# A block of attention, experts and two hybrid layers: 512-column products with an identity, at the edges of stages

## The reference

```python
def first_block(x, ...):
    z = rms_norm(x, norm1_g) @ w_in
    y_nsa = nsa_attention(...)        # compressed, selected and windowed keys
    y_dil = dilated_attention(...)
    x = x + (gate0 * (y_nsa @ w_up_nsa) + gate1 * (y_dil @ w_up_dil)) @ w_o
    return x + peer(rms_norm(x, norm2_g), ...)      # experts

def hybrid_layer(x, ...):             # twice
    proj = rms_norm_2(x, n_pre_mix) @ w_in
    y_a, y_b, y_c = pool_mixer(...) @ w_a, gla_mixer(...) @ w_b, mla_mixer(...) @ w_c
    merged = gates[0] * y_a + gates[1] * y_b + gates[2] * y_c
    x = x + rms_norm_2(merged @ w_o, n_post_mix)
    gu = rms_norm_2(x, n_pre_ffn) @ w_ffn_gu
    ffn = (silu(gu[..., :D_FF]) * gu[..., D_FF:]) @ w_ffn_down
    return x + rms_norm_2(ffn, n_post_ffn)
```

## Time and profile before

| | |
|---|---|
| median of 3 runs | 3793.26 us (3791.05 to 3793.95) |
| profiled execution | 3793.5 us |
| its span, first to last instruction | 3791.7 us |
| mean granted TensorE clock | 0.969 |
| TensorE busy | 3584.7 us (95%) |
| VectorE busy | 2367.3 us (62%) |
| ScalarE busy | 1422.4 us (38%) |
| GpSimd busy | 391.9 us (10%) |

### The profile page before, as it was taken

One profiled execution on the slowest core, in us unless ns is written; L12 is line 12 of the kernel. 1 busy time (PEld: TensorE's weight loads), 2 busy tenths in 40 slices (PEclk: granted clock), 3 DMA queues, 4 the chain that ended last, 5 costly groups with the idle time before them and its releaser, 6 DMA issues. The chain is left out here.

```text
span 3791.7 us, 47619 instructions
## 1 busy us (share of the span) xinstructions
PE 3584.7 (95%) x18126; PEld 3069.5 (81%) x18133; DVE 2367.3 (62%) x4248; ACT 1422.4 (38%) x2386; POOL 391.9 (10%) x309
## 2 busy tenths in 40 slices
PE   8988999999999899999998989999999898999998
PEld 6666777999999899999886767788878676778886
DVE  3376664889999888888635556554343545564433
ACT  3234343434799543333323324332222322443221
POOL 0020000000244433333000100000000010000000
PEclk9999999999999999999998999999999998999999
DMA  3220232555799999999432224233323222333332
GB/s 129 81 78 23 73 123 84 177 170 174 262 380 379 392 347 381 373 365 368 159 101 69 80 62 136 84 100 100 94 74 100 73 78 59 123 103 92 98 94 70
DMA packets 212358, 597.86 MB, mean 158 GB/s; under 512 B 21730, under 2 KB 79748, under 8 KB 210596
## 3 DMA queue, kind: packets, MB, share of 16 engines
q1 hardware_dynamic: 175268, 460.58, 36.8%
q0 software_dynamic: 36864, 134.23, 9.2%
HBM read 525.00 MB, written 69.21 MB: 157 GB/s over the span
## 5 line engine op out<-in xcount | busy, mean ns | idle before, releaser
L653 ACT ACTIVATE stream_hi<-stream_raw 128x1024 fp32r<-128x1024 f32 (+1 forms) x615 | 642.7, 1045 | 1204.3 <-PE ffn_ps L2773 416.8
L661 DVE TENSOR_TENSOR stream_lo<-stream_raw,stream_hi 128x1024 fp32r<-128x1024 f32 (+1 forms) x615 | 745.1, 1212 | 401.9 <-ACT stream_hi L653 393.2
L1231 PE MATMUL experts_ps<-mix_a_hi,stream_hi 128*128 128x384 f32 x1024 | 342.8, 335 | 18.2 <-issue 16.8
L689 PE MATMUL experts_ps<-h_hi,stream_hi 128*128 128x384 f32 x1024 | 347.9, 340 | 1.5 <-PEq L101 1.5
L689 PE MATMUL experts_ps<-h_hi,stream_lo 128*128 128x384 f32 x1024 | 343.1, 335 | 0.0
L689 PE MATMUL experts_ps<-h_lo,stream_hi 128*128 128x384 f32 x1024 | 343.1, 335 | 0.0
L1231 PE MATMUL experts_ps<-mix_a_lo,stream_hi 128*128 128x384 f32 x1024 | 342.6, 335 | 0.0
L1231 PE MATMUL experts_ps<-mix_a_hi,stream_lo 128*128 128x384 f32 x1024 | 342.5, 334 | 0.0
L2771 PE MATMUL mid_ps<-h_hi,stream_hi 128*128 128x512 f32 x672 | 286.2, 426 | 20.2 <-DVE h_lo L2800 17.1
L2771 PE MATMUL ffn_ps<-h_hi,stream_hi 128*128 128x512 f32 x704 | 283.4, 402 | 17.7 <-DVE h_lo L2800 17.7
L2773 PE MATMUL ffn_ps<-h_hi,stream_lo 128*128 128x512 f32 x704 | 275.4, 391 | 0.0
(11 more groups left out here) (465 smaller groups left out, 7115.5 us busy)
## 6 DMA issues: line engine op xcount, KB each, us to landing
stream_raw<-u SPq DMA_DIRECT2D x128, 512.0 KB
stream_raw<-v SPq DMA_DIRECT2D x128, 512.0 KB
stream_raw<-l_gu SPq DMA_DIRECT2D x88, 512.0 KB
expert_hidden<-experts_gelu SPq DMA_DIRECT2D x128, 192.0 KB
expert_weights<-built SPq DMA_DIRECT2D x12, 2048.0 KB
built<-expert_weights SPq DMA_DIRECT2D x16, 1536.0 KB
built<-expert_hidden SPq DMA_DIRECT2D x128, 192.0 KB
stream_raw<-l_gate SPq DMA_DIRECT2D x48, 512.0 KB
```

The lines of the kernel that those rows point to most:

```text
L653: self.nc.scalar.activation(self.hi[n % self.RING][:, 0:w], self.raw[n % self.RAW][:, 0:w], ACT.Copy).then_inc(self.hi_done, 1)
L661: self.nc.vector.tensor_tensor(self.lo[n % self.RING][:, 0:w], self.raw[n % self.RAW][:, 0:w], self.hi[n % self.RING][:, 0:w].bitcast(F32) ...
L689: mm = self.nc.tensor.matmul(self.ps[n % 2], a, b[:, k, :], start=(k == 0 and m == 0), stop=(k == DC - 1 and m == 2))
L1231: mm = nc.tensor.matmul(out[d][:, DIRECT:SEQ], v, a[b % RING][:, :], start=(b == 0 and m == 0), stop=(b == KEYS - 1 and m == 2))
```

## The change

A new function multiplies the bf16 identity, repeated four times along the free dimension, by the bf16 identity into one bank of PSUM, n times: each product is 128x128 by 128x512. It waits for nothing and raises no semaphore. It is called on TensorE at seven places of the code. `paired_attention` is used twice, and the others once for each of two layers, so the calls run at 14 places, with 183 products in all. The banks are `turned[0]` of the attentions, and banks 3, 6, 2, 5 and 2 of the other stages; what is written there is not read: the next product into them starts anew.

```diff
@@ paired_attention, tensor
                 score(0)
+                idle_products(nc, C, turned[0], 10)
                 for n in range(N):
...
                     mix(n, chunks[n] - 1)
+                idle_products(nc, C, turned[0], 8)
@@ after three
+def idle_products(nc, C, out, n):
+
+    of = C.mask_ident.unsqueeze(1).to_broadcast([P, 4, P])
+    for _ in range(n):
+        nc.tensor.matmul(out.rearrange("p (a c) -> p a c", a=4), C.mask_ident, of, start=True, stop=True)
@@ project, tensor
+                idle_products(nc, C, bank[3], 14 if res.adds else 9)
                 res.first_two(pe, stream, first, bank, total)
@@ merge_and_out, tensor
             def _(pe):
+                idle_products(nc, C, bank[6], 12)
                 for n in range(N_UP):
...
                 leave.total(pe, total)
+                idle_products(nc, C, bank[2], 18)
@@ ffn, tensor
             def _(pe):
+                idle_products(nc, C, bank[5], 14)
                 res.first_two(pe, stream, first, bank, x_total)
...
                 leave.total(pe, m_total)
+                idle_products(nc, C, bank[2], 18)
```

## The result

| | before | after |
|---|---|---|
| median (range, executions) | 3793.61 us (3791.05 to 3798.87, 4) | 3773.79 us (3769.47 to 3775.02, 4) |
| profiled execution | 3793.5 us | 3774.04 us |
| its span | 3791.7 us | 3772.2 us |
| mean granted TensorE clock | 0.969 | 0.979 |

The ratio (changed kernel over kernel before) is 0.9944, 95% interval 0.9931 to 0.9956: faster by 0.56%, 19.8 us on the medians. The prediction said 3781.5 (3775 to 3791).

What follows compares the result with a forecast made beforehand. TensorE, busy 95%, was taken to bound the kernel, losing time to waits and the lower clock. Terms -12.9 + 0.4 + 3.0 - 1.9 - 0.7 + 0.4 = -11.7 from 3793.5 gave 3781.8, stated as 3781.5 us, range 3775 to 3791.

Steps and rivals of the forecast that it cites:

- Starts of merge, feed-forward and second projection: Five stage openings: products hidden in the waits win back the lost clock, 5 x 2.57 = 12.9 us gained, bounds 8.4 and 15.2.
- hidden ends: Four ends of merge and feed-forward: 18 products hidden behind VectorE's reciprocal with no margin, 0.1 us each, +0.4 in all.
- mean of all nine edges: Clock loss in the 8 us after work resumes, averaged: 23.12 / 9 = 2.57 us, used for each of five entries.
- Ends of the attentions: Ends of dil and nsa: nothing covers the 8 products, the next stage starts later, +1.5 us each, +3.0.
- First scores: Waits inside the paired attentions' first scores, ten products each: nsa gains 1.9 us, dil 0.7 (bounds +1.0 and -2.3).
- +1.0 of delay: dil's first scores: ten products at 0.43 us take 4.3 against a wait of 3.31, delaying the next scores by 1.0.
- Start of the first projection: First layer's projection: nine products at the lower clock delay by 2.2 us against at most 2.24 won back; +0.4.
- identity products don't hold the clock: Rival for all edges: clock falls as before and products run at the lower level, +20.5 us, 3814 us; chance 0.10.
- partial: Rival: end products delay each barrier about 1 us, merges' entry sometimes still cold; -2.5, 3791 us; chance 0.15.
- moderate case: Rival: edges at the low bound, 8.4, or first projection and dil at their upper bound; -7.2, 3786 us; chance 0.17.

Runs made afterwards that it cites:

- mixers_later: Kernel before plus 16 identity products at the end of both layers' projections, to start the mixers 2.8 us later; 3799.05 us.
- five_entries: Changed kernel with only the calls at starts and ends of merge and feed-forward and the second projection's start; 3776.91 us, ratio 0.9951.
- mixers_shifted: Changed kernel plus 7 identity products at the end of both projections, to put off the mixers' stages by some 0.8 us; 3781.27 us.
- gla_later: Kernel before plus five unneeded VectorE operations at the end of the first layer's projection, no identity products; 3795.80 us.
- ends_only: Changed kernel with only the 18 products at the ends of merge and feed-forward; 3787.34 us.
- starts_only: Changed kernel without the products at the ends of the attentions, merges and feed-forwards; 3775.79 us.
- no_attention_ends: Changed kernel without the 8 products at the ends of dil and nsa; 3772.52 us, ratio 0.9942.
- before_again: Kernel before, unchanged, run for a second profile; 3795.89 us.
- attentions_only: Changed kernel with only the calls in the two paired attentions, 36 products; 3795.53 us.
- more_edges_2: Changed kernel without products at the attentions' ends, with products at many further edges, up's end and latent's last rotation included; 3753.10 us, ratio 0.9882, one execution 6812.76 us.

## Why the prediction was right in its sign and wrong in its size

**The step that failed** is the sum itself. It adds what happens at the 14 places and has no term for stages that the change doesn't touch: it takes a stage's loss to the lower clock as a property of its waits. The mixers' two stages gave 5.5 of the 7.8 us that the forecast lacks; dil and the first projection lie 0.9 and 0.8 below their terms, and the rest is spread in amounts of 0.2. mixers_later shows the gain without the edits, five_entries shows it in the one layer that is moved and not in the other, and mixers_shifted takes it away again in the second layer while every edit stays. That the traces of before could have told it is only half true: they show 27.31 us of lower clock in both layers' mixers, which looks like a fixed price.

The traces of all runs without products inside the mixers tell how place and loss go together: how far into the stage the clock first falls goes with the loss in all 21 such stages (11 runs with two each, but for the first layer of gla_later, where the clock was low from the start), edits or none:

| first fall, us into the stage | stages | at the lower level, us | length of the stage, us |
|---|---|---|---|
| 43.2 to 44.0 | 10 | 27.31 | 111.95 to 112.68 |
| 44.4 to 44.8 | 9 | 20.48 | 109.49 to 109.95 |
| 45.3 to 45.4 | 2 | 13.65 | 107.07 to 107.17 |

TensorE's wait for `gla_att` runs from 41.5 to 45.0 us in both kernels' traces. So the gain of 5.5 us is real but was luck of place: nothing in the change aims at it, ends_only has half of it without an edit ahead, and mixers_shifted loses half of it with all edits in place.

**Starts of merge, feed-forward and second projection.** Forecast -12.9, and +0.4 for the hidden ends; measured -12.6 (five_entries: -12.7). Right, and so were its signs: clock 1.00 in all five, 0.81 us behind the reciprocal. Edge by edge, the losses read from the earlier trace rows (2.56 and 2.72 for the merges, 2.96 and 3.04 for the feed-forwards, 2.16 for the projection) came back but for 3 to 8%: 2.39 and 2.51, 2.78 and 2.84, 2.09. They add up to 13.4; that the mean of all nine edges gave 12.9 and so lay nearer is a little luck. Also right was to cost start and end products together. Neither half does it alone at the 8.8 us waits: the ends alone won 0.0, the starts alone 0.95 and 1.15 of 2.8 and 0.6 of 2.1. At the 4.3 us wait ahead of the merge the starts alone do all.

**Ends of the attentions.** Forecast +1.5 each; measured 1.39 and 1.51. They bought nothing in return.

**First scores.** nsa forecast -1.9; 178.15 to 176.00 without the end products is -2.15. dil was mis-sized: forecast -0.7, measured -1.44 (70.16 to 68.72). The term that failed is the +1.0 of delay, from ten products at 0.43 each: the clock was up after 1.1 us of them, they took 2.87 us instead of 4.3 and ended 0.65 us before the next scores could start (lines below, of the changed kernel). With the ends the two come to -0.7 where the sum had +0.4.

```profile
276.31 2.87 PE L2782 MATMUL first_ps<-masks_sb 128*128 128x512 bf16 x10
279.83 1.48 PE L390 MATMUL first_ps<-z 64*128 64x512 f32 x6 [0.65 <-ACT dil_probs L505]
```

**Start of the first projection.** Forecast +0.4; -0.39 between the two profiles, which isn't clear of chance: the stage took 133.7 to 134.2 us in the three traces with its nine products (after, starts_only, no_attention_ends) and 133.3 to 134.5 in the five without any product in it (before, before_again, five_entries, attentions_only, ends_only). The first real product comes 3.32 us behind ScalarE's first operation (1864.82 to 1868.14) instead of 1.65, so 1.7 of delay where the text has 2.2, against the 2.24 of lost clock, all of which came back (0.72 to 1.00):

```profile
1864.82 0.72 ACT L2818 ACTIVATE h_hi<-x_sb,stream_gains 128x512 fp32r<-128x512 f32 x1 [10.12 <-PEq L101]
1864.84 3.65 PE L2782 MATMUL mid_ps<-stream_masks 128*128 128x512 bf16 x9 [6.25 <-PEq L101]
...
1868.14 0.58 PE L2773 MATMUL mid_ps<-h_hi,stream_hi 128*128 128x512 f32 x1
```

**The rivals.** That identity products don't hold the clock is refuted by the eight edges at 1.00. The partial and the moderate case didn't occur. The case that did, a gain above the forecast through stages that only move, was not among them, and the range's lower end (3775) had room only for better prices at the same places.

**What stays open.** Whether the nine products of the first projection win anything. What sets the moments at which the clock changes isn't shown; only that a move of the stage's start changes the loss, by 2.6 to 2.8 us a step, and that places with 27.31, 20.48 and 13.65 us of lower clock all occur. The long execution of more_edges_2 isn't explained.

## What to carry to other kernels

Where TensorE bounds and the stages' openings run at the lower clock, products that nobody reads, placed in waits that other engines set anyway, win the lost half speed back: 12.6 us at five entries here, in a result of 0.56% of which 5.5 us come from stages that merely moved, and 1.2% in all when further edges get them too. Check that another engine's work covers each call (behind the last copy of the attentions nothing did, 1.4 us each), and fill a long wait from both sides. Read the result stage by stage with the lower clock of each: a change that moves later stages by a microsecond or two can win or lose 2.7 us in a stage that it doesn't touch, and neither is evidence for or against the edit.

## What was not expected of the hardware

- The loss at one wait isn't fixed. The same 430 products of the mixers' stage took 112.6, 109.8 or 107.1 us, at a granted clock of 0.88, 0.91 and 0.94, by where the stage began.
- Almost all elements of these products are zero, and the clock stayed at 1.00 over them: the 8.84 us from the last total to the first real product, with 32 identity products and two gaps of 1.0 and 0.7 us, in the changed kernel:

```profile
2427.67:2436.51 8.84, 7.07 (x34) 2.90 (x31) 7.26 (x8) 2.67 (x5) 0.00 (x0) 1.00 0.00 1
```

- With 18 products ahead of it and none behind, the same wait still cost a feed-forward's opening its full 2.8 us (380.01 us against 380.04).
